# Experts as plain single precision products on four column strips, with unsplit weights in eight buffers and 32x32 block transposes of the activations

## The reference, cut to what matters

```python
def swiglu(h, w1, w3, w2):
    a = jax.nn.silu(jnp.einsum('bsd,df->bsf', h, w1)) * jnp.einsum('bsd,df->bsf', h, w3)
    return jnp.einsum('bsf,fd->bsd', a, w2)

    logits = jnp.einsum('bsd,de->bse', h, w_router).astype(jnp.float32)
    top_val, top_idx = lax.top_k(logits, TOP_K)
    top_gate = jax.nn.softmax(top_val, axis=-1)
    ...
    for e in range(N_EXPERTS):
        y = y + gates[..., e:e + 1] * swiglu(h, w1[e], w3[e], w2[e])
```

## Time and profile before

| | |
|---|---|
| median of 3 runs | 1456.19 us (1454.39 to 1458.1) |
| profiled execution, span of its instructions | 1452.6 us |
| TensorE busy | 1438.3 us, 99% |
| VectorE, ScalarE busy | 1131.9 us, 942.6 us |
| bytes moved | 437.28 MB, mean 301 GB/s |
| experts' stage | from about 486 us to the end |

### The profile page before, as it was taken

The page is one execution under the profiler, slowest core; times in us unless marked ns, Lnnn a source line. Parts: engine busy times, 40 slices in busy tenths (PEclk is TensorE's granted clock), DMA queues, the critical chain, the costliest instruction groups (busy, mean ns, idle before and its releaser), DMA issues.

```text
span 1452.6 us, 19103 instructions
## 1 busy us (share of the span) xinstructions
PE 1438.3 (99%) x7542; PEld 1198.0 (82%) x7542; DVE 1131.9 (78%) x968; ACT 942.6 (65%) x844; POOL 41.2 (3%) x22
## 2 busy tenths in 40 slices
PE   9999999999999999999999999999999999999998
PEld 7998888888886788888887888888888888888886
DVE  6984764445476798889887898988888888888795
ACT  7634643343376767777776777777777777777674
POOL 0000000000000000000000001001000000000100
PEclk9999999999999999999999999999999999999999
DMA  9610665553443399999999999999999999999994
GB/s 360 210 59 16 247 216 210 203 180 144 158 156 112 135 379 390 378 375 387 368 364 369 384 393 375 397 373 386 384 375 375 396 364 375 382 370 379 373 382 163
DMA packets 134726, 437.28 MB, mean 301 GB/s; under 512 B 4880, under 2 KB 6416, under 8 KB 134672
## 3 DMA queue, kind: packets, MB, share of 16 engines
q1 hardware_dynamic: 131344, 426.11, 77.9%
q0 software_dynamic: 2336, 8.39, 2.2%
q10 hardware_dynamic: 992, 2.05, 0.4%
HBM read 431.29 MB, written 5.24 MB: 301 GB/s over the span
## 4 chain that ended last, share of the span: by engine, by line
PE 66%; DMA 14%; issue 9%; DVE 8%; ACT 3%; POOL 0%; DVEq 0%; POOLq 0%; SPq 0%; ACTq 0%
PE ps L272 20%; PE ps L274 20%; PE ps L273 20%; DMA raw<-in_od_moe_w 13%; DVE wlo L261 5%; ACT whi L255 2%; DMA out<-arena,slot_tok 1%; PE ps L460 1%; PE ps L999 1%; PE ps L1196 0%; PE ps L333 0%; DVE small L1425 0%; PE ps L1571 0%; DVE hTlo L316 0%; DMA xres<-in_x 0%
## 5 line engine op out<-in xcount | busy, mean ns | idle before, releaser
L261 DVE TENSOR_TENSOR wlo<-raw,whi 128x2048 fp32r<-128x2048 f32 x406 | 905.9, 2272 | 168.7 <-ACT whi L255 167.0
L255 ACT CAST whi<-raw 128x2048 fp32r<-128x2048 f32 x406 | 750.4, 1898 | 228.3 <-DMA raw<-in_od_moe_w 161.4
L272 PE MATMUL ps<-whi,hThi 128*128 128x512 f32 (+1 forms) x1240 | 485.9, 392 | 0.5 <-DVE hTlo L316 0.3
L274 PE MATMUL ps<-whi,hTlo 128*128 128x512 f32 (+1 forms) x1240 | 481.2, 388 | 0.0
L273 PE MATMUL ps<-wlo,hThi 128*128 128x512 f32 (+1 forms) x1240 | 481.1, 388 | 0.0
L272 PEld LDWEIGHTS ps<-whi,hThi 128*128 128x128 f32 x1240 | 232.9, 188 | 48.6 <-issue 1.1
L274 PEld LDWEIGHTS ps<-whi,hTlo 128*128 128x128 f32 x1240 | 232.8, 188 | 48.2
L273 PEld LDWEIGHTS ps<-wlo,hThi 128*128 128x128 f32 x1240 | 233.0, 188 | 46.2 <-issue 0.2
L272 PE MATMUL ps<-whi,aThi 128*128 128x512 f32 x560 | 222.2, 397 | 0.0
L274 PE MATMUL ps<-whi,aTlo 128*128 128x512 f32 x560 | 218.5, 390 | 0.0
L273 PE MATMUL ps<-wlo,aThi 128*128 128x512 f32 x560 | 218.1, 389 | 0.0
(11 more groups left out here) (308 smaller groups left out, 765.2 us busy)
## 6 DMA issues: line engine op xcount, KB each, us to landing
raw<-in_od_moe_w SPq DMA_DIRECT2D x168, 2048.0 KB, 10.0
raw<-in_ev_ffn_w SPq DMA_DIRECT2D x21, 2048.0 KB, 7.8
raw<-in_ev_w_in SPq DMA_DIRECT2D x6, 2048.0 KB, 13.5
raw<-in_ev_w_out SPq DMA_DIRECT2D x2, 2048.0 KB, 8.4
raw<-in_od_w_in SPq DMA_DIRECT2D x2, 2048.0 KB, 7.7
raw<-in_od_w_out SPq DMA_DIRECT2D x2, 2048.0 KB, 8.1
raw<-in_ev_w_in SPq DMA_DIRECT2D x2, 1024.0 KB, 7.6
xres<-in_x SPq DMA_DIRECT2D x2, 512.0 KB, 4.5
```

The source lines that it names most:

```text
L255: act.copy(whi[s][:, part], raw[s][:, part]).then_inc(hi_ready, 1)
L261: dve.tensor_tensor(wlo[s][:, part], raw[s][:, part], whi[s][:, part].bitcast(F32), ALU.subtract).then_inc(lo_ready, 1)
L272: pe.matmul(to, lhi, rhi, start=first, stop=False)
L274: return pe.matmul(to, llo, rhi, start=False, stop=last)
```

## The change

Parts of the diff. The expert products no longer use split weights. Stationary are 32 slots (`strip(g)`, three groups) and the array is used in four column strips of 32 columns, `strip(j)`, each with its own moved columns of the weights in plain `F32` and its own 32 partitions of the same bank. Upward a strip takes 448 of the 1792 columns of a block (two blocks per expert, `SB`), in runs of 32 with stride 128; downward it takes 256 of the 1024 output columns. The weight buffers are `raw0` to `raw2` and five of the six that held `whi` and `wlo`, which lie in the same memory; an upward unit is 2 row blocks by 1792 columns (1.84 MB), a downward one 4 row blocks by 1024 columns (2 MB, the fourth half of it). A load waits for TensorE's use of the unit eight before it. ScalarE and VectorE split nothing; silu and gating work on 128 partitions x 448 columns for each slot group, and VectorE's 32x32 block transposes, which take the place of TensorE's, leave the activations with the contraction on the partitions. The dense first block and `gather_silu` are gone. The order on TensorE is: upward block 0, downward block 1 of the expert before, upward block 1, downward block 0. GpSimd issues a gather before the scatter that it stood behind. A product with a zeroed operand (`zero_r`) clears the shared output bank.

```diff
+NB = 8
+SB = 2
+SBW = F // SB
+STRIPS = 4
+SW = P // STRIPS
+SG = CAP // SW
+SN = SBW // STRIPS
+YN = D // STRIPS
+SC = SBW // P
+UP_UNITS = KD
+DOWN_UNITS = -(-SC // 4)
+U_PASS = NE * SB * (UP_UNITS + DOWN_UNITS)
...
-        whi = [sb(f"whi{s}", [P, UNIT], F32R) for s in range(NS)]
-        wlo = [sb(f"wlo{s}", [P, UNIT], F32R) for s in range(NS)]
+        whi, wlo, wide = [], [], []
+        for s in range(NS):
+            for parts, name in ((whi, f"whi{s}"), (wlo, f"wlo{s}")):
+                wide.append(sb(f"wide_{name}", [P, UNIT]))
+                parts.append(nc.alloc_sbuf_tensor_at(name, [P, UNIT], F32R, offset=nc.sbuf_base - 4 * UNIT))
...
-            first_loads(sp, U_MOE, moe_col(w1m, 0), moe_col(w3m, 0), third=moe_wide(w1m, 0, 1, 0))
...
+            act.activation(zero_r, ident, ACT.Copy, scale=0.0).then_inc(mask_ready, 1)
...
-            hi_u(act, U_MOE)
...
+        W = raw + wide[0:NB - NS]
+        w_full = raw_full + sem("w_full3 w_full4 w_full5 w_full6 w_full7")
+        W_FREE = {3: U_MOE - 2, 4: U_MOE - 2, 5: U_MOE - 1, 6: U_MOE - 1, 7: U_MOE}
+        xT = ar(4640, KD, CAP)
+        aT = [ar(7232 + SG * SN * n, SG, SN) for n in range(SB)]
+        H1S, H3S = ps[0:SG], ps[SG:2 * SG]
+        YS = [ps[6][:, 0:YN], ps[6][:, YN:2 * YN], ps[7][:, 0:YN]]
...
+            def put(q, e, at, k, n, source):
+                s, u = buffer(e, at), unit(q, e, at)
+                if q == 0 and is_at(e, 0) and at < NB:
+                    if at < NS:
+                        sp.wait_ge(lo_ready, 2 * (u - NS + 1))
+                    else:
+                        sp.wait_ge(unit_used, W_FREE[at])
+                else:
+                    sp.wait_ge(unit_used, u - NB + 1)
+                sp.dma_start(weights(s, k, n), source).then_inc(w_full[s], 16)
+
+            def up(q, e, b):
+                for i in range(UP_UNITS):
+                    w, k0 = (w1m, w3m)[i // 4], 2 * (i % 4)
+                    put(q, e, up_at(e, b) + i, 2, SBW, w[bass.ds(e, 1), :, k0:k0 + 2, SBW * b:SBW * b + SBW].rearrange(
+                        "e p k n -> p (e k) n"))
+
+            def down(q, e, b):
+                x, at = down_at(e, b)
+                for i in range(DOWN_UNITS):
+                    c0, n = SC * b + 4 * i, down_rows(i)
+                    put(q, x, at + i, n, D, w2m[bass.ds(e, 1), :, c0:c0 + n, :].rearrange("e p c n -> p (e c) n"))
+
+            def expert(q, e):
+                up(q, e, 0)
+                if not is_at(e, 0):
+                    down(q, e - 1, 1)
+                up(q, e, 1)
+                down(q, e, 0)
...
+                gather(n0 + 1)
                 for n in range(n0, n0 + NE - 1):
-                    gather(n + 1)
+                    if n + 2 < n0 + NE:
+                        gather(n + 2)
...
+                act.copy(xT[:, 0:4, :], by_slot(FIRST[0])).then_inc(xT_ready, 1)
+
+            def silu(q, e, b):
+                act.wait_ge(unit_used, unit(q, e, up_at(e, b) + UP_UNITS // 2))
+                m = blocks(q, e, b)
+                for g in range(SG):
+                    if not is_at(m, 0):
+                        act.wait_ge(h_gated, SG * m - SG + g + 1)
+                    act.activation(silu3[:, g], H1S[g][:, 0:SN], ACT.Silu).then_inc(h_sil, 1)
...
+            def activations(q, e, b):
+                m = blocks(q, e, b)
+                dve.wait_ge(unit_used, unit(q, e, up_at(e, b) + UP_UNITS))
+                for g in range(SG):
+                    dve.wait_ge(h_sil, SG * m + g + 1)
+                    if not is_at(m, 0):
+                        dve.wait_ge(aT_turned, SG * m - SG + g + 1)
+                    dve.tensor_tensor(gated[:, g], silu3[:, g], H3S[g][:, 0:SN], ALU.mult).then_inc(h_gated, 1)
+                for g in range(SG):
+                    dve.wait_ge(h_gated, SG * m + g + 1)
+                    dve.transpose(aT[b][:, g], gated[:, g]).then_inc(aT_turned, 1)
...
+            def expert_out(q, e):
+                n = NE * q + e
+                x, at = down_at(e, 1)
+                dve.wait_ge(gate_ready, n + 1)
+                dve.wait_ge(unit_used, unit(q, x, at + DOWN_UNITS))
+                dve.wait_ge(sc_sent, 16 * n + 16)
+                for g in range(SG):
+                    for j in (2, 3):
+                        dve.tensor_scalar(ys[strip(g), YN * j:YN * j + YN], YS[g][strip(j)],
+                                          slot_gate[strip(g), bass.ds(n, 1)], None, ALU.mult).then_inc(ys_ready, 1)
...
+            def last_out(q):
+                n = NE * q + NE - 1
+                dve.wait_ge(gate_ready, n + 1)
+                dve.wait_ge(old_in, 16 * q + 16)
+                for g in range(SG):
+                    if g < SG - 1:
+                        dve.wait_ge(y_group, (SG - 1) * q + g + 1)
+                    else:
+                        dve.wait_ge(unit_used, U_MOE + U_PASS * (q + 1))
+                    for j in range(STRIPS):
+                        col = slice(YN * j, YN * j + YN)
+                        dve.scalar_tensor_tensor(ys[strip(g), col], Y_LAST[g][strip(j)], slot_gate[strip(g), n:n + 1],
+                                                 xg[strip(g), col], ALU.mult, ALU.add).then_inc(ys_ready, 1)
...
-            def dense(t, ks):
-
-                wh, wl = band(whi[0], KD, GW), band(wlo[0], KD, GW)
-                tok = slice(t * P, t * P + P)
-                for k in ks:
-                    if t == 0 and k % 4 == 0:
-                        pe.wait_ge(lo_ready, 2 * U_MOE + k // 4 + 1)
-                    ins = product(pe, H1[t][:, :], hThi[:, k, tok], hTlo[:, k, tok], wh[:, k], wl[:, k],
-                                  k == 0, k == KD - 1)
-                return ins
...
-                if b < 3:
-                    dense(0, (2 * b, 2 * b + 1))
...
-            dense(0, (6, 7))
...
-            dense(1, early)
...
-            dense(1, late).then_inc(unit_used, 1)
...
+            def up(q, e, b, units=range(UP_UNITS)):
+                m = blocks(q, e, b)
+                for i in units:
+                    at = up_at(e, b) + i
+                    s = buffer(e, at)
+                    w = weights(s, 2, SBW).rearrange("p k (b j i) -> p k j b i", j=STRIPS, i=SW)
+                    to = (H1S, H3S)[i // 4]
+                    if i % 4 == 0 and not is_at(m, 0):
+                        pe.wait_ge((h_sil, h_gated)[i // 4], SG * m)
+                    pe.wait_ge(w_full[s], 16 * fills(q, e, at))
+                    for kk in range(2):
+                        k = 2 * (i % 4) + kk
+                        for g in range(SG):
+                            for j in range(STRIPS):
+                                ins = pe.matmul(to[g][strip(j), 0:SN].rearrange("p (b i) -> p b i", i=SW),
+                                                xT[:, k, strip(g)], w[:, kk, j], start=k == 0, stop=k == KD - 1)
+                    ins.then_inc(unit_used, 1)
...
+            def down(q, e, b, units=range(DOWN_UNITS), last=False):
+                x, at = down_at(e, b)
+                to, shared = (Y_LAST, ()) if is_at(e, NE - 1) else (YS, (0, 1))
+                if shared and b == 0 and 0 in units:
+                    pe.matmul(ps[6][:, :].rearrange("p (h k) -> p h k", h=2), zero_r,
+                              over_heads(mask_r.rearrange("p a i -> p (a i)"), 2), start=True, stop=False)
+                for i in units:
+                    s = buffer(x, at + i)
+                    w = weights(s, down_rows(i), D)
+                    pe.wait_ge(w_full[s], 16 * fills(q, x, at + i))
+                    final = last and i == DOWN_UNITS - 1
+                    order = [(c, g) for c in range(down_rows(i)) for g in range(SG)]
+                    for c, g in sorted(order, key=lambda cg: cg[1]) if final else order:
+                        cc = 4 * i + c
+                        if cc == 0:
+                            pe.wait_ge(aT_turned, SG * blocks(q, e, b) + g + 1)
+                        for j in range(STRIPS):
+                            ins = pe.matmul(to[g][strip(j)], aT[b][:, g, SW * cc:SW * cc + SW],
+                                            w[:, c, YN * j:YN * j + YN],
+                                            start=b == 0 and cc == 0 and g not in shared, stop=b == SB - 1 and cc == SC - 1 and not (shared and g == 0))
+                        if final and c == down_rows(i) - 1 and g < SG - 1:
+                            ins.then_inc(y_group, 1)
+                    ins.then_inc(unit_used, 1)
...
+                pe.wait_ge(xT_ready, 2 * n + 2)
+                up(q, e, 0)
+                if not is_at(e, 0):
+                    down(q, e - 1, 1)
+                up(q, e, 1, range(UP_UNITS // 2))
+                if not is_at(n, 0):
+                    pe.wait_ge(ys_ready, SG * STRIPS * n)
+                if not is_at(e, NE - 1):
+                    index(q, e + 1)
+                up(q, e, 1, range(UP_UNITS // 2, UP_UNITS))
+                if is_at(e, NE - 1):
```

(56 more changed lines are left out.)

405 lines of the change are left out of this document (87 added, 318 removed).

## The result

The changed kernel takes 1440.78 us (median of 4 runs, 1439.34 to 1442.98), the kernel before 1456.66 beside it: ratio 0.9892, 95% interval 0.9875 to 0.9909. Faster, clear of the noise, but by 16 us, where 46 were forecast. The profiled execution has a span of 1437.5 us, against 1452.6.

What follows compares the result with a forecast made beforehand. TensorE set the pace by about 1% over a full transfer ring. After the change: ring 1394 + 11 = 1405, TensorE 1387.7 + 7.3 = 1395; later one plus 1: span 1406, plus 3.6: 1410 us, range 1392 to 1458.

Steps and rivals of the forecast that it cites:

- eight transposes and the index product (0.9), the zeroing product (0.25), and some four changes between strip and full form ...: 110.0 us: TensorE's floor per expert: 108.5 us of packs plus these leftovers gives 110.0, against 117.1 before.
- At 390 GB/s: 882 us, so 1394: Weight transfers after the start: 343.9 MB left at an assumed 390 GB/s, last landing at 1394 us.
- the ring: The sixteen DMA engines' transfers, taken as the later limit: 1394 + 11 = 1405 us, against TensorE's 1395.
- No loss of clock is charged after the start: TensorE in the experts' stage: idle moments spread, about 0.2 us per unit, so no low clock charged.
- The start: Routing to first upward product: at 506 us, as before; gather 5.3 us (3.7 before), first packs lose 1.7.
- The end: After TensorE's last product: 7.3 us to the span's end; 10.5 to 11 after the last landing.
- The pack's price: Four column strips running fully at once: 376 ns per pack upward, 216 ns downward.
- Rivals 2 and 3: 2: strips not fully at once, 1627 to 2267 us, 0.20; 3: pack 8-18 ns dearer, 1422-1451, 0.14 with Rival 4.
- What costs nothing: Silu, gating and block transposes, 4 to 6 us per block, hidden under a downward block of 17 to 18 us.
- Rival 1: Transfers keep 378 GB/s in the experts' stage: 1437 us, chance 0.22.
- Rival 4: A wait serializes upward and downward blocks, 16 x 2 us or more: 1440 and up, chance 0.14 together with rival 3.
- TensorE waits for the weights' transfers for about 10 us: Expected sign in the profile: TensorE's total wait for weights about 10 us or more, DMA share 1.00.

Runs made afterwards that it cites:

- last experiment: Changed kernel with TensorE's loop written out, ten idle products in routing, gate values before the gathered copy, last downward block ordered by slot groups: 1394.67 us, ratio 0.9598.

## Why the prediction was wrong in size

1. **The step that failed: "eight transposes and the index product (0.9), the zeroing product (0.25), and some four changes between strip and full form ...: 110.0 us" per expert.** The work in it was right (110.56 where nothing else stood in the way), but the sum held only work. The change turns 504 products into 720 calls of two loads and two records, 1144 instructions into 2933; the loop no longer fits what TensorE holds, and each of five turns pays 5.1 to 5.4 us of refetching and 1.3 to 2.6 of low clock: 35.6 us. I had counted the records to price them and did not ask where they come from. The branch at 208 ns in the kernel before could not show it; the rule cited above of the Trainium skill could have warned of it.
2. **"At 390 GB/s: 882 us, so 1394"**, and with it the ring as the later of two limits: refuted. The ring can do 410 (1373.76 us with half the products). The steady 378 of the earlier trace rows was then not its limit, in spite of a share of 1.00; rows of 4 KB as there come at 410 here. That it was the pace of TensorE (117.1 of 118.5 us) and the split fits, but no run takes TensorE out of the way in the kernel before. The forecast took the ring's sum, the later of the two; TensorE's was the one to take. That eight buffers are needed for the rate is refuted too (four: 403 to 409).
3. **"No loss of clock is charged after the start"**: wrong, and it follows from 1. Waits of up to 1.2 us left the granted clock at 1.00 in each 200 us window (four buffers, 700 to 1300 us); five standstills of 5 us did not.
4. **The start**: mechanism right (the gather at the low level), mis-sized: 7.0 for 5.3 us, 2.3 us in all with the later start. Ten added products bring the gather back to 3.7. The first packs' 1.7 is right: the first 144 packs take 55.84 us, 1.7 more than 144 x 376 ns.
5. **The end**: 9.9 for 7.3 us. I took the last group's four operations as all that stands behind the last product; ordering only the last unit by groups leaves more. With the whole last block in that order (last experiment) the end is 8.3 us: 1.6 saved, where I expected 4.
6. **The pack's price**: right to the nanosecond: 96 packs in 36.08 us, 376 each; 84 downward in 18.13, 216 each. Rivals 2 and 3 fall. The records of a plain product over the full array (the added ones: six in 2.74 us, each 0.59 long) come 429 ns apart for 512 columns, 0.84 ns a column; a pack's 376 for 448 is 0.84 too. So four strips, each with its own 448 columns, take the time of one product. By the Trainium skill's ratio ("TensorE: Matmul & The Clock Gate", "Measured speedup vs the span model": 2.38 for three strips) four would be worth an estimated 3.17 and lose a fifth; here four strips are worth four, and no run has three.
7. **What costs nothing**: right. No wait of TensorE for VectorE or ScalarE stands in 560 to 1300 us; the three 32x32 block transposes take 0.60 us each.
8. **Rival 1** gave 1437 and the kernel took 1440.78, but by another mechanism: the stage's 381 GB/s is a mean over a ring at 400 and a ring that stands still. The window after 1300 tells them apart; the total does not. **Rival 4**'s serializing wait does not exist.
9. **"TensorE waits for the weights' transfers for about 10 us"**: it waits 0 us for them, the sign, in the profile itself, that the ring is not the limit.

## What to carry to other kernels

Count an engine's instructions per turn of a loop before and after a change, not only their time: where the body outgrows what the engine holds (on TensorE here between 1589 and 1829 instructions), write the loop out, or keep the body under it. A steady transfer rate beside a busy engine is no measure of the ring, even at a share of 1.00: take the engine's work away and look. When two limits are close, a total that fits one of them proves nothing; the waits do.

## What the runs showed of the hardware

- In the strip kernels with bodies of 1829 to 2933 instructions a taken jump back of TensorE puts 5.3 to 6.9 us between products (0.2 without a jump), and 5.9 to 7.6 in the branch's record; in the kernel before with bodies of 2290 and 3417 it is 1.7 to 5.2 us, and 3.9 to 6.6. With bodies of 1144 and 1589 the branch takes 208 ns, and untaken 76 to 83. Straight code of the same length costs nothing visible at 12 packets of 16 KB per 118 us.
- Behind a standstill of 5.4 us the granted clock is 0.50 for another 2.7 to 5.2 us (changed kernel).
- Transfers of 1.8 and 2 MB keep 408 to 411 GB/s over hundreds of microseconds on one core; rows of 7 KB 420, rows of 4 KB 410.
- Four column strips of 32 take as long per moved column as one plain product over the full array (0.84 ns).
- Products of 2 columns, one behind the other for 41 us, come with a granted clock of 0.55, though TensorE counts as busy throughout.
- Open: the jump's greater length in the run with ten more products ahead and its spread from 1.7 to 6.9 us between kernels, the exact limit and what sets it, and the rest of the 10 us that longer bodies cost the kernel before.
